# Seventeen of thirty modulation vectors: from TensorE matmuls over 1 MB slabs to row sums on VectorE over 512 KB pieces

## What is computed

```python
silu_c = jax.nn.silu(c)
silu_cc = jax.nn.silu(c_ctx)
for l in range(DEPTH):
    m_lat = (silu_c @ w_mod[l] + b_mod[l]).reshape(Bsz, N_MOD, 1, D)   # N_MOD = 9, D = 1024
    m_ctx = (silu_cc @ w_mod[l] + b_mod[l]).reshape(N_MOD, D)
    x = x + 0.5 * m_lat[:, 2] * swiglu(modulate(rms_norm(x), m_lat[:, 0], m_lat[:, 1]), ffn_in[l, 0], ffn_out[l, 0])
    ...
```

## Time and profile before

| | |
|---|---|
| median of 3 runs | 3808.41 us |
| span of the profiled execution | 3809.4 us |
| PE busy | 3587.4 us, 94% |
| DVE busy | 1836.3 us, 48% |
| ACT busy | 1418.9 us, 37% |
| DMA from SyncE's queue | 441.68 MB, 34.6% of 16 engines |

### The profile page before, as it was taken

How to read it: one execution, slowest core, us unless ns; L and a number is a source line. 1 busy time by engine, 2 the same in 40 slices (tenths; PEclk the granted TensorE clock), 3 DMA queues, 4 the chain that set the end, 5 groups by cost and what they waited for, 6 DMA issues and landing times.

```text
span 3809.4 us, 62156 instructions
## 1 busy us (share of the span) xinstructions
PE 3587.4 (94%) x27294; PEld 2960.9 (78%) x27294; DVE 1836.3 (48%) x3143; ACT 1418.9 (37%) x2303; POOL 60.0 (2%) x98
## 2 busy tenths in 40 slices
PE   6999999888889999999987999999999989999898
PEld 4777885677668888877874998777887768879898
DVE  2223445666654233423265553654464443566575
ACT  3123334434334222323244543443243332445553
POOL 0000000000010000000000000020000000010000
PEclk8999999999999999999998999999999999999999
DMA  5454123222243233243225552121324552223463
GB/s 194 163 183 134 59 83 127 102 102 102 102 77 110 91 99 100 90 142 122 89 89 212 174 180 96 58 78 56 100 83 172 177 173 93 89 91 127 145 190 113
DMA packets 257918, 453.93 MB, mean 119 GB/s; under 512 B 14096, under 2 KB 157584, under 8 KB 243184
## 3 DMA queue, kind: packets, MB, share of 16 engines
q1 hardware_dynamic: 253840, 441.68, 34.6%
q0 software_dynamic: 3808, 8.27, 1.3%
HBM read 447.24 MB, written 1.94 MB: 118 GB/s over the span
## 4 chain that ended last, share of the span: by engine, by line
PE 81%; DVE 10%; ACT 4%; DMA 3%; issue 1%; SPq 0%; DVEq 0%; ACTq 0%
PE bank L1072 80%; DVE W L1859 2%; DVE W L1868 2%; DVE WR L1859 2%; DMA ring<-in_w_mod 1%; ACT WR L1524 1%; ACT W L1524 1%; PE bank L1295 1%; DMA ring<-in_w_up 1%; DVE H L1859 1%; DVE HL L1859 1%; DMA ring<-in_w_ada 1%; DVE X L1868 0%; ACT H L1524 0%; DVE small L2136 0%
## 5 line engine op out<-in xcount | busy, mean ns | idle before, releaser
L1072 PE MATMUL bank<-HH,WR 128*128 128x512 f32 (+1 forms) x9312 | 2430.9, 347 | 74.9 <-DVE WR L1859 42.0
L1072 PEld LDWEIGHTS bank<-HH,WR 128*128 128x128 f32 x9312 | 1643.3, 192 | 334.3 <-DVE WR L1859 54.4
L1072 PE MATMUL bank<-HL,WR 128*128 128x512 f32 (+1 forms) x4656 | 1601.3, 344 | 0.0
L1859 DVE TENSOR_TENSOR WR<-ring,WR 128x2048 fp32r<-128x2048 f32 (+3 forms) x300 | 673.8, 2250 | 859.9 <-ACT WR L1524 859.4
L1524 ACT ACTIVATE WR<-ring 128x2048 fp32r<-128x2048 f32 (+3 forms) x300 | 562.6, 1881 | 1200.1 <-PE bank L1072 819.5
L1072 PEld LDWEIGHTS bank<-HL,WR 128*128 128x128 f32 x4656 | 895.4, 192 | 96.9
L1524 ACT ACTIVATE W<-bank 64x256 f32<-64x256 f32 (+4 forms) x662 | 285.8, 442 | 388.6 <-PE bank L1072 342.1
L1072 PE MATMUL bank<-W 64*64 64x64 f32 (+5 forms) x6304 | 351.7, 247 | 41.4 <-ACT W L1524 20.5
L1072 PEld LDWEIGHTS bank<-W 64*64 64x64 f32 (+3 forms) x6304 | 266.1, 140 | 131.6 <-issue 47.2
L1868 DVE SCALAR_TENSOR_TENSOR W<-bank,vec,W 128x510 f32<-128x510 f32 (+1 forms) x206 | 130.6, 634 | 190.2 <-ACT W L1524 186.6
L1524 ACT ACTIVATE W<-bank,small 128x512 f32<-128x512 f32 (+2 forms) x183 | 113.1, 622 | 225.8 <-DVE small L2136 154.1
(11 more groups left out here) (111 smaller groups left out, 2022.0 us busy)
## 6 DMA issues: line engine op xcount, KB each, us to landing
ring<-in_ffn_in SPq DMA_DIRECT2D x176, 512.0 KB, 5.0
ring<-in_w_mod SPq DMA_DIRECT2D x72, 1024.0 KB, 5.4
ring<-in_w_in SPq DMA_DIRECT2D x52, 1024.0 KB, 5.1
ring<-in_w_ada SPq DMA_DIRECT2D x48, 1024.0 KB, 6.5
ring<-in_ffn_out SPq DMA_DIRECT2D x176, 256.0 KB, 3.6
ring<-in_w_up SPq DMA_DIRECT2D x88, 512.0 KB, 5.0
ring<-in_w_down SPq DMA_DIRECT2D x88, 256.0 KB, 3.6
ring<-in_even_w_in SPq DMA_DIRECT2D x8, 1024.0 KB, 5.1
```

The lines of the kernel that those rows point to most:

```text
L1072: return e.matmul(o, l, r, start=start, stop=stop, skip_group_check=True)
L1859: put(e.tensor_tensor(o, a, b, op), *events)
```

## The change

For 17 vectors (m0 2 to 8, m1 0 to 5, a0 0 to 3) VectorE now sums the rows: a piece is 128 rows x 1024 columns of the weights (512 KB), and per piece one operation for each conditioning (nv = 2; for m1 5 only one) multiplies it by the row's silu and adds it to ACC. After 8 pieces TensorE sums ACC over partitions with a matrix of ones (rows_sum), ScalarE copies the result, and rows_tr turns it. The two raw silu vectors are taken in place at the start (begin).

Pieces live in one ring buffer, two halves of 1024 columns, that rows_begin takes out of turn for the whole feed-forward; the weights have the other two. They are loaded by SyncE in the order of SLABS, between the weight slabs, and each waits for the sum of the piece that was in its half. They run in f00, 2 and f10: 40, 40 and 32 pieces in the input half at 0.55 per column block, and 8 at 0.9 in each output half. The modulation slabs of f00, f10, the LoRA stretch, 24 of 36 in wkv and 8 of 16 in the odd mixer are gone. Smaller edits: bank reuse after a broadcast waits 8 takes instead of 6, silc is filled by a copy, G's columns from 18 on wait for the sum whose ACC lies there.

```diff
         MROW = {}
+        SILU = {n: Vc(n, 0, 16) for n in ("cc", "cc2")}
+        ACC = [[wv(25088, [1024]), wv(27136, [1024])], [wv(9216, [1024]), wv(10240, [1024])]]
...
 
+        def rows_begin():
+
+            i = hold["keep"] = (hold["slot"] + 1) % NS
+            hold["halves"] = [IN_SLOT[i], IN_SLOT[i]]
+
+        def rows_end():
+            hold["slot"], hold["keep"], hold["halves"] = hold["keep"], None, None
+
+        def rows_slab(w, k, idx):
+
+            i, h = hold["keep"], k % 2
+            SLABS.append(dict(parts=[w[P * k:P * k + P, 1024 * idx:1024 * idx + 1024]], kc=1, w=1024, kind="rows", half=h,
+                              split_from=hold["split"], slots=hold["slots"], ring=i, before=hold["halves"][h],
+                              n=sum(x["kind"] == "split" for x in SLABS)))
+            IN_SLOT[i] = hold["halves"][h] = len(SLABS) - 1
+            return IN_SLOT[i]
+
         def slot(s):
             return ring[SLABS[s]["ring"]]
+
+        def rows_of(s):
+            h = SLABS[s]["half"]
+            return slot(s).rearrange("p k c -> p (k c)")[:, 1024 * h:1024 * h + 1024]
 
         def landed(s):
...
+                        if each:
+                            each()
                     if between:
...
+                if k in (1, 4) and PENDING:
+                    ORDER.append(PENDING.pop(0))
...
-        PREVIOUS = {"m1": ("m0", 4), "a0": ("m1", 4), "a1": ("a0", 2)}
-
-        def columns(t):
+        PREVIOUS = {"a0": ("m1", 4)}
+        PENDING = []
+
+        def columns(t, blocks):
 
 
             w, n, *_ = TABLES[t]
-            ORDER.append(("silu_c", t))
-            for b in range((n + 2047) // 2048):
+            if t in ("m0", "a0"):
+                ORDER.append(("silu_c", t))
+            for b in blocks:
                 nc_ = min(2048, n - 2048 * b)
                 ks = 2048 // nc_
...
-        tick = [0.0]
+        def row_sums(jobs, buf):
+
+            tail = []
+            for t, idx, nv in jobs:
+                for k in range(KD):
+                    s = rows_slab(TABLES[t][0], k, idx)
+                    ORDER.append(("rows", t, idx, k, s, nv, buf))
+                    if tail and k in (2, 4):
+                        ORDER.append(tail.pop(0))
+                    yield
+                tail = [("rows_sum", t, idx, s, nv, buf), ("rows_tr", t, idx, nv)]
+                buf = 1 - buf
+            PENDING.extend(tail)
+
+        def now(steps_):
+            ORDER.extend(steps_)
+            del steps_[:]
 
         def background(gen, rate):
-            tick[0] = 0.0
+            tick = [0.0]
 
             def step():
                 tick[0] += rate
...
-        def ffn(name, w_in, w_out, i0, ntok, mod, after, bg=None):
+        def ffn(name, w_in, w_out, i0, ntok, mod, after, bg=None, rows=None):
             modnorm("n" + name, ntok, mod, i0, i0 + 1)
             groups = [[g * 256, g * 256 + P, FF + g * 256, FF + g * 256 + P] for g in range(11)]
+            if rows:
+                rows_begin()
             lin(name + "i", "ffn_in", w_in, groups, KD, ntok, ready="n" + name,
-                between=background(*bg) if bg else None)
+                between=background(*bg) if bg else None, each=background(rows[0], rows[1]) if rows else None)
             for _ in bg[0] if bg else ():
                 pass
-            lin_deep(name + "o", w_out, G, ntok, mod, i0 + 2, after, name + "i")
+            if rows:
+                for _ in rows[0]:
+                    pass
+                now(PENDING)
+            lin_deep(name + "o", w_out, G, ntok, mod, i0 + 2, after, name + "i",
+                     each=background(rows[2], rows[3]) if rows else None)
+            if rows:
+                for _ in rows[2]:
+                    pass
+                rows_end()
 
 
         EQ, EK = wv(0, [4, 512]), wv(2048, [512])
...
-        cols = {t: columns(t) for t in TABLES}
+        cols = {"m0": columns("m0", [0]), "m1": columns("m1", [3, 4]), "a0": columns("a0", [2]), "a1": columns("a1", [0, 1, 2])}
...
         ORDER.append(("split_next",))
-        ffn("f00", A["ffn_in"][0, 0], A["ffn_out"][0, 0], 0, NT, 0, "ne", (itertools.islice(cols["m0"], 18), 0.85))
+        pairs_of = lambda t, a, b, nv=2: [(t, idx, nv) for idx in range(a, b)]
+        ffn("f00", A["ffn_in"][0, 0], A["ffn_out"][0, 0], 0, NT, 0, "ne",
+            rows=(row_sums(pairs_of("m0", 2, 7), 0), 0.55, row_sums(pairs_of("m0", 7, 8), 0), 0.9))
         even_mixer(cols["m0"], cols["m1"])
-        ffn("2", A["ffn_in"][0, 1], A["ffn_out"][0, 1], 6, NT, 0, "nf10", (skewed(), 0.2))
-        ffn("f10", A["ffn_in"][1, 0], A["ffn_out"][1, 0], 0, NT, 1, "no", (itertools.islice(cols["a0"], 9), 0.5))
+        ffn("2", A["ffn_in"][0, 1], A["ffn_out"][0, 1], 6, NT, 0, "nf10", (skewed(), 0.2),
+            rows=(row_sums(pairs_of("m0", 8, 9) + pairs_of("m1", 0, 4), 0), 0.55, row_sums(pairs_of("m1", 4, 5), 0), 0.9))
...
+            if step[0] == "rows":
+                use[step[4]] = i
...
-        befores = lambda s, kind: [x["before"] for x in SLABS[:s + 1] if x["before"] is not None and SLABS[x["before"]]["kind"] == kind]
+        befores = lambda s, *kinds: [x["before"] for x in SLABS[:s + 1] if x["before"] is not None and SLABS[x["before"]]["kind"] in kinds]
...
+            if step[0] == "rows":
+                assert not todo or todo[0] not in befores(step[4], "split")
...
-                    if any(use[r] >= i for r in befores(todo[0], "raw")):
+                    if any(use[r] >= i for r in befores(todo[0], "raw", "rows")):
...
                            C("sel", 0, 2 * nb, 0, 32 * nb), True, True)
+                x.then_inc(MM.sem, MM.mark(key))
+                shut(key)
+
+            def rows_sum(t, idx, s, nv, buf):
+                key = ("rows", t, idx)
+                o = take(key)
+                q.wait_ge(IN["first"], ("in", "first"))
+                q.wait_ge(DVES, ("rows", s))
+                for j in range(2):
+                    for v in range(nv):
+                        i = 32 * (nv * j + v)
+                        x = mm(o[i:i + 32, :], C("ones", 0, 32), ACC[buf][v][:, 512 * j:512 * j + 512], True, True)
+                x.then_inc(MM.sem, MM.mark(key))
+                shut(key)
+
+            def rows_tr(t, idx, nv):
+                key = ("rowsc", t, idx)
+                n = 2 * nv
+                q.wait_ge(ACTS, ("mrow", t, "rows", idx))
+                o = take(key)
+                for m in range(4):
+                    x = mm(o[:, n * m:n * m + n], RROW[0:32 * n, m * P:(m + 1) * P], C("sel", 0, 2 * n, 0, 32 * n)[:, ::2], True, True)
                 x.then_inc(MM.sem, MM.mark(key))
                 shut(key)
...
-                q.wait_ge(IN["vec"], ("in", "vec"))
+                q.wait_ge(ACTS, ("silu", src))
                 q.wait_ge(DVES, ("silc_zero",))
                 if t in PREVIOUS:
                     q.wait_ge(MM, ("mod", *PREVIOUS[t]))
-                act(silc[:, :, 0:2], Vc(src, 0, 16).rearrange("p (h k) -> p k h", h=2), ACT.Silu, ("silc", t))
+                act(silc[:, :, 0:2], SILU[src].rearrange("p (h k) -> p k h", h=2), ACT.Copy, ("silc", src))
+
+            def begin():
+                q.wait_ge(IN["vec"], ("in", "vec"))
+                for src, to in SILU.items():
+                    act(to, to, ACT.Silu, ("silu", src))
+
+            def rows_sum(t, idx, s, nv, buf):
+                key, n = ("rows", t, idx), 64 * nv
+                q.wait_ge(MM, key)
+                act(RROW[0:n, :], banks[BANK.get(key, 0)][0:n, :], ACT.Copy, ("mrow", t, "rows", idx), ("free", key))
 
             def mod_mm(t, b, k0, ks, nb, s):
...
+            def rows(t, idx, k, s, nv, buf):
+                src = TABLES[t][3]
+                q.wait_ge(ROWS[SLABS[s]["half"]], ("raw", s))
+                q.wait_ge(ACTS, ("silu", src))
+                if k == 0:
+                    if FREED[buf] is not None:
+                        q.wait_ge(MM, FREED[buf])
+                    FREED[buf] = ("rows", t, idx)
+                for v in range(nv):
+                    c = SILU[src][:, 8 * v + k:8 * v + k + 1]
+                    events = [("rows", t, idx, k, v)] + ([("rows", s)] if v == nv - 1 else [])
+                    if k == 0:
+                        ts(ACC[buf][v], rows_of(s), c, None, ALU.mult, None, *events)
+                    else:
+                        q.wait_ge(DVES, ("rows", t, idx, k - 1, v))
+                        stt(ACC[buf][v], rows_of(s), c, ACC[buf][v], ALU.mult, ALU.add, *events)
+
+            FREED = [None, None]
...
+                    elif SLABS[x["before"]]["kind"] == "raw":
+                        q.wait_ge(MM, ("used", x["before"]))
                     else:
-                        q.wait_ge(MM, ("used", x["before"]))
+                        q.wait_ge(DVES, ("rows", x["before"]))
                 for w, k0, c0 in x["parts"]:
                     kc, n = w.shape[0] // P, w.shape[1]
                     if n > 512:
```

(10 more changed lines are left out.)

51 lines of the change are left out of this document (40 added, 11 removed).

## The result

The changed kernel takes **4081.58 us** (median of 4 runs, 4073.18 to 4093.59) against 3812.62 us for the kernel before in the same comparison (3801.29 to 3818.58): ratio 1.0713, 95% interval 1.0687 to 1.0738. It is 7.1% slower, 20 us above the forecast of 4062. Its profiled execution has a span of 4087.3 us.

The account below looks back on a forecast made before the run. TensorE, busy 94% of the span, was taken to bound the kernel. Losses of 95 + 95 + 64 + 60 + 8 + 12 = 334 us less 80 saved gave +254 and 4062 us, range 3930 to 4170.

Parts of the forecast that it names:

- T = 17.0 us: Gated slabs of the input halves: landing 6.9, 1.95, lo 2.21, 2.2 pieces of 2.42, products 0.64, against 10.89 us.
- 199 + 83 + 12: Input halves of f00 and f2: 18 gated slabs, 36 pieces, 9 groups of products; loss 95 us each.
- 95 + 20 + 8 + 4 - 19: f00: input half, output half, delayed constant load and closing sums added, savings taken off; +108 us.
- f10's loss of 64: f10's input half: 8 pieces of one operation, 24 of two, 14 gated slabs; 227 us against TensorE's 163.
- The even mixer's 40: Savings from removed modulation passes: 18 us in the LoRA stretch (5 to 26), 22 in wkv (5 to 35).
- The constants' 8 us in f00: f00: the 2208 KB constant load in the same queue now delays a gated slab by about 8 us.
- The output halves: Three feed-forwards' output halves: 17.5 us lost at the second slab, 2.5 at the third; 20 each, 60 in all.
- The closing sums: End of each feed-forward half: rows_sum, copy and rows_tr wait for ScalarE; about 4 us a feed-forward, 12 in all.
- rival C: TensorE's clock stays at 1.2 GHz through each slab: 21.8 us per slab, 240 us more, 4300 us; 4%.
- Rival A: Landing lies under cover and only VectorE's 8.2 us of load count, so nothing is lost: 3740 us; 7%.
- Rival B: A gate is passed one piece sooner, pieces lie inside the landing: T = 11.7 us, 3830 us in all; 6%.
- Signs that I had named: f2's input half: hi 17 us apart, released by DMA; TensorE waits 4 to 6 us; VectorE some 60% busy; then 10.9.

Follow-up runs that it names:

- x_no_pieces: Changed kernel without the pieces, their sums and the closing sums; modulation products read ones, the TensorE column blocks stay removed: 3732.83 us, ratio 0.9798.
- x_lo2: Changed kernel with its SyncE queue kept and each slab's lower half two pieces' sums later in VectorE's order: 4019.54 us, ratio 1.0553.
- x_pool_skew: x_pool_queue with GpSimd's 16 bias-table copies issued before f2 begins instead of between its pieces: 3768.91 us, ratio 0.9898.
- x_pool_queue: Changed kernel with pieces issued by GpSimd, weights alone on SyncE, and splits no longer held behind pieces' sums: 3792.98 us, ratio 0.9963.
- x_one_sum: Changed kernel with one sum per piece instead of two, the second vector's sums left out: 4008.12 us, ratio 1.0516.
- x_pool_one_sum: x_pool_skew with one sum per piece instead of two: 3768.18 us, ratio 0.9896.
- x_slab_first: Changed kernel with each weight slab ahead, in SyncE's queue, of the pieces made since the slab before it: 4028.5 us, ratio 1.0574.
- x_lo_later: Changed kernel with each slab's lower half one piece's sums later in VectorE's order: 3966.08 us, ratio 1.0415.

## Why the prediction was right

**The period.** The mechanism was right: a cycle through SyncE's queue and VectorE's order, not load. T = 17.0 us was the step that decided, and f2 shows 17.0. Its parts stand in the rows: gate to hi 6.9 in the cycle shown, hi to lo 1.95, a piece 2.43 (4.87 for two) against 2.42. Some of the exact agreement is luck. The 7.87 and 9.12 us were counted from the issue of the modulation slab ahead; from the slab's own issue it is 7.5 and 8.7. The landing from issue to hi is 6.7 us on average over f2's 18 slabs, not 6.9, and the 0.4 us between the gate's end and the issue, which the sum left out, makes up for it. And the sum did not use 17.0: 199 + 83 + 12 for 18 slabs is 16.3 each, 12 us less over a half than 17.0 gives. As f2 as a whole came out within 1 us, the other terms must be some 11 us too high; the output half is 3 of them (17.0 for 20), the rest isn't assigned. scalar_tensor_tensor of 128x1024 takes 1279 ns against 1.28 us from the step between the earlier trace rows's widths, so the growth by 530 ns from 512 to 1024 columns carried over between the two operations. The first operation of a block takes 747 ns against 0.75. The formula (N+151)/0.96 of the Trainium skill, VectorE: DVE Perf Modes, section on the TRN2 errata, gives, as an estimate, 1224 ns for 1024 columns: near the 1222 of tensor_tensor in the earlier trace rows, 55 ns low for this operation.

**By stage** (predicted, measured from the marks). f00: 95 + 20 + 8 + 4 - 19 = +108, +100.5. f2: 95 + 20 + 4 = +119, +120.2. f10: 64 + 20 + 4 - 10 = +78, +92.3. Even mixer: -40, -25.0. Rest: -11, -10.0. The sum is off by 24 us, and two steps carry it:

- *f10's loss of 64.* With the savings taken off by x_no_pieces (369.0), its pieces cost 103 us, not 88. The step counted a piece of one operation at half a piece and nothing else. With so short a piece VectorE gets ahead, and the gate sum then can stand behind products that wait for TensorE (2.13 and 2.03 us). In the kernel after:

```profile
1784.55 0.69 DVE L1959 TENSOR_TENSOR W<-W,bank 128x512 f32<-128x512 f32 x1 [2.03 <-PE bank L1140]
1785.15 1.28 DVE L1968 SCALAR_TENSOR_TENSOR W<-ring,vec,W 128x1024 f32<-128x1024 f32 x1
...
1793.41 1.92 ACT L1614 ACTIVATE WR<-ring 128x2048 fp32r<-128x2048 f32 x1 [13.70 <-DMA ring<-in_ffn_in]
```

  The hi before it was at 1774.26, so this cycle took 19.2 us with one operation per piece, more than the 17.0 with two. It is the longest of three; the next two took 14.6 and 17.9 us (the last with a third piece in it). Over the half, f10's slabs were issued 17.4 us apart (1766.09 to 1992.14 in 13) where the sum had 221 / 14 = 15.8. That is 21 us over 13 spacings, enough for the 15; how it divides between products that wait and longer landings isn't shown.
- *The even mixer's 40.* x_no_pieces gives 32.7; LoRA and wkv yield less than their passes, as the lower bounds allowed. The other 7.7 us are not the pieces': x_lo2 and x_pool_skew have them and take 690.5 and 692.2 us, as little as x_no_pieces. They are mostly the granted clock. The same matmuls, without a wait between, take 17.7 us in x_no_pieces (591.92 to 609.62), 18.1 in x_pool_skew (608.50 to 626.61), 23.2 in x_pool_queue (608.05 to 631.25) and 23.8 in the changed kernel (718.15 to 741.99). The windows of 20 us there, x_pool_queue and x_pool_skew, show a clock of 0.70 and 0.97:

```profile
614.65:634.65 20.00, 18.00 (x79) 8.97 (x78) 9.45 (x25) 8.41 (x20) 0.00 (x0) 0.70 0.00 0
...
614.68:634.68 20.00, 17.08 (x99) 8.44 (x97) 11.52 (x31) 11.03 (x26) 0.00 (x0) 0.97 0.00 1
```

  The four kernels of 697 to 701 us (after, x_one_sum, x_pool_queue, x_pool_one_sum) have 0.67 to 0.70 in this window, all others with the change 0.97 to 1.00. Why the clock differs isn't shown; each kernel has one trace, so it may be the execution and not the kernel. The constants' 8 us in f00 was not tried by itself.

**The output halves** were put at 17.5 us for the second slab, from a landing of 3.4 us and two sums a piece. TensorE's longest waits in the three output halves were 17.1, 17.0 and 17.7. Moving the slabs ahead in x_slab_first took 45.7 us off the three feed-forwards (53 in all), for the 60 of the sum, and waits of 2.5 and 2.8 us are left there.

**The closing sums** were put at 12 us because most of them were to lie in TensorE's new waits. In the changed kernel that may be so; where the waits are gone they cost 24. That step can be right only for a kernel that is already slow.

**The clock.** The granted clock in the gated stretches is 0.87 to 0.88, against 1.00 in the earlier trace rows. TensorE was ready before each lo all the same (waits of 3.4 and 3.2 us before the slabs at 1308 and 1324), so the cycle hides it, and rival C, at 21.8 us a slab, didn't come. Behind the wait at 1308.31 a pair of matmuls takes 1.06 us until 1311.5 and 0.62 from then on; behind that at 1324.23 the first take 0.62 to 0.71 us a pair and only those from 1325.3 to 1328.3 are slow. The price is nil as long as something else is later. By the Trainium skill, TensorE: Matmul & The Clock Gate, section HAM oscillation, each tile behind a DMA wait starts at the low clock. The trace agrees at 1308.31; at 1324.23 the low clock comes 1 us behind the start.

**Rival A** had the right size in the wrong kernel: 3740 against 3769 for x_pool_skew. I priced it as what happens if the landing lies under cover, and it does once the order allows it. **Rival B**'s condition (lo behind piece p-1) was built as x_lo_later, which gave 14.0 us a slab and 3966, not 11.7 and 3830. That rival was mis-sized. It took all 2.2 pieces out of the cycle, but moving lo by one piece takes one out.

**Signs that I had named.** The hi copies are 17 us apart and released by the DMA, as said. TensorE's waits for WR are 259.0 us in 65, 4.0 each. The period is back at 10.9 once the pieces end (hi at 2027.63 and 2038.51 in f10). VectorE is busy 46% in f2's stretch (132.16 of 290 us), not "some 60%": my own 8.2 us in 17.0 make 48%, so the text had contradicted its sum. Behind f10 the time is 10.0 us shorter, for the odd mixer's 11; wkv by itself wasn't read.

## What to carry to other kernels

When a new transfer joins an in-order queue, ask for each later transfer what it now waits for, and whether that waits, in some engine's program order, for the later transfer itself. If it does, the length of that cycle is the period, whatever the engines' loads are: here 17.0 us against 10.9, with 8.2 us of VectorE's work in it. To cut such a cycle, change both orders or give the new transfer a queue of its own and free the other engine's order to match; moving one order alone gave 53, 62 or 116 us where both gave 287. And look at what else stands in the program you move to: 16 small copies between the pieces cost another 24 us (21.4 of them in f2), as the next piece couldn't be issued before the last of them.

## What I had not expected of the hardware

Small copies can hold up large ones far beyond their bytes, and whatever stands behind them in their engine's program. The 16 bias-table copies are under 1 MB, and around them a 512 KB DMA of SyncE's took 24.5 us (median of four) instead of 4.8, with the DMA share shown at 1.10 and 1.04 for 20 us while only 83 and 67 GB/s moved (windows of x_pool_queue at 1230 to 1250). The loss itself came by the other way, GpSimd's stop of 26.59 us ahead of the sixteenth copy:

```profile
1230.00:1240.00 10.00, 10.00 (x45) 8.27 (x45) 3.03 (x4) 0.00 (x0) 2.35 (x3) 1.00 1.10 83
1240.00:1250.00 10.00, 10.00 (x45) 8.26 (x45) 0.00 (x0) 0.00 (x0) 0.00 (x0) 1.00 1.04 67
```

That GpSimd issues a 512 KB DMA in 0.53 us, so that 136 of them added only 72 us to its 60 us of busy time (131.8 us in x_pool_skew), was welcome: that engine was free.
